# Modulation weights in quarters through two places of their own, a ring of five, a later turn of branch a

## The reference, cut to what matters

```
h = x @ w_in[i]                       # ua va za q k v zb ga gb, 18 column blocks of 512
ya = ua * sa * silu(za)               # branch a: a causal 128x128 mix over tokens
yb = rms(diff_attention(q, k, v)) * silu(zb)
merged = sigmoid(ga) * (ya @ w_branch_a) + sigmoid(gb) * (yb @ w_branch_b)
x = layer_norm(ALPHA * x + merged @ w_out + sigmoid(x @ w_ple_gate) * (p @ w_ple))
# second block: six modulation vectors of 1024 come from silu(c) @ w_mod + b_mod
# (1024 x 6144); attention with latents and with forget gates, then a mixture
# of 64 experts (6 a token) and a shared expert
```

## Time and profile before

| | us |
|---|---|
| median of 3 runs | 1123.41 (1122.72 to 1124.83) |
| the profiled execution, device time | 1123.09 |
| its span, first to last instruction | 1121.3 |
| TensorE busy, mean granted clock | 1059.9, 0.976 |
| VectorE, ScalarE, GpSimd busy | 546.5, 390.3, 338.4 |

### The profile page before, as it was taken

One profiled execution on the slowest core, in us unless ns is written; L12 is line 12 of the kernel. 1 busy time (PEld: TensorE's weight loads), 2 busy tenths in 40 slices (PEclk: granted clock), 3 DMA queues, 4 the chain that ended last, 5 costly groups with the idle time before them and its releaser, 6 DMA issues. The chain is left out here.

```text
span 1121.3 us, 12888 instructions
## 1 busy us (share of the span) xinstructions
PE 1059.9 (95%) x5022; PEld 705.2 (63%) x5022; DVE 546.5 (49%) x986; ACT 390.3 (35%) x677; POOL 338.4 (30%) x261
## 2 busy tenths in 40 slices
PE   6999999979999899799899999999999999999993
PEld 4888888868887787687678545444535354444442
DVE  5969676758757775855555222222222222212214
ACT  4645575446433654465233111111111111111112
POOL 1058965596486005918900000000000000000000
PEclk9999999989999899899999999999999999999997
DMA  9656654856766464454359499999999999999981
GB/s 328 209 175 243 215 188 147 315 174 224 247 216 210 153 195 155 166 171 148 113 216 414 192 392 412 420 416 417 416 416 418 417 418 416 416 417 417 417 362 39
DMA packets 93933, 320.65 MB, mean 286 GB/s; under 512 B 6288, under 2 KB 7328, under 8 KB 76976
## 3 DMA queue, kind: packets, MB, share of 16 engines
q1 hardware_dynamic: 92832, 316.07, 73.8%
q0 software_dynamic: 752, 3.22, 0.8%
q10 hardware_dynamic: 288, 0.52, 0.1%
HBM read 318.74 MB, written 1.05 MB: 285 GB/s over the span
## 5 line engine op out<-in xcount | busy, mean ns | idle before, releaser
L803 PE MATMUL ps<-hl,L 128*128 128x512 f32 (+1 forms) x1216 | 388.3, 401 | 14.4 <-DVE rlo L1615 8.5
L803 PEld LDWEIGHTS ps<-hl,L 128*128 128x128 f32 x1216 | 231.5, 193 | 63.7 <-issue 15.7
L1615 DVE TENSOR_TENSOR rlo<-ring,hl 128x1024 fp32r<-128x1024 f32 (+1 forms) x154 | 206.2, 1359 | 113.7 <-ACT hl L1241 113.3
L803 PE MATMUL ps<-rlo,L 128*128 128x512 f32 (+1 forms) x608 | 241.1, 396 | 0.0
L803 PE MATMUL ps<-slots_all,xe 128*64 128x512 f32 (+1 forms) x1056 | 226.9, 582 | 0.8 <-DVE rt L2406 0.8
L1241 ACT ACTIVATE hl<-ring 128x1024 fp32r<-128x1024 f32 (+1 forms) x154 | 158.8, 1055 | 182.5 <-PE ps L803 73.3
L764 POOL TENSOR_SCALAR ring<-ring,st 128x512 f32<-128x512 f32 x84 | 171.0, 2036 | 0.0
L792 POOL CAST two<-ident 64x128 fp32r<-64x128 f32 x64 | 18.7, 292 | 476.4 <-PE ps L803 440.7
L803 PEld LDWEIGHTS ps<-slots_all,xe 128*64 128x64 f32 x1056 | 73.9, 137 | 131.7 <-issue 128.5
L803 PEld LDWEIGHTS ps<-rlo,L 128*128 128x128 f32 x608 | 117.1, 193 | 24.9
L766 POOL TENSOR_TENSOR macc<-macc,ring 128x512 f32<-128x512 f32 x84 | 120.1, 1430 | 7.0
(11 more groups left out here) (210 smaller groups left out, 905.0 us busy)
## 6 DMA issues: line engine op xcount, KB each, us to landing
slots_all<-in_w_exp_gate SPq DMA_DIRECT2D x64, 1024.0 KB, 19.8
slots_all<-in_w_exp_up SPq DMA_DIRECT2D x64, 1024.0 KB, 15.8
slots_all<-in_w_exp_down SPq DMA_DIRECT2D x64, 1024.0 KB, 16.6
ring<-in_w_in SPq DMA_DIRECT2D x49, 1024.0 KB, 5.5
ring<-in_w_mod SPq DMA_DIRECT2D x24, 1024.0 KB, 5.2
ring<-in_w_out SPq DMA_DIRECT2D x8, 1024.0 KB, 5.1
ring<-in_w_ple_gate SPq DMA_DIRECT2D x4, 1024.0 KB, 5.1
ring<-in_w_branch_a SPq DMA_DIRECT2D x4, 1024.0 KB, 6.6
```

Source lines behind the costliest of these rows:

```text
L803: return e.matmul(o, l, r, start=start, stop=stop)
L1615: return e.tensor_tensor(o, a, b, op)
```

## The change

It takes the 24 modulation loads out of the ring's list. The ring has five places; the sixth becomes `mring`, two places of 512 KB. GpSimd queues the modulation weights itself, in 48 quarters of 512 KB (two rows of K), the next one into a place once its sums have left it. `MOD_SUM` is written out: most sums come one or two blocks earlier, part 11's from the end of the dense part to `om0`. The list of waits of GpSimd (the mask of `ws`, the second load of x into `rbuf`, the gates' bias) is hung on the parts 6, 8 and 5. Branch a is turned after `ga0` on all engines. The second load of `q0` comes in halves too, with a quarter of x ahead of each half, and the side job of the set-up starts after piece 4 and not piece 2. Five of the nine loads of constants wait for x's second quarter. TensorE starts with 12 matmuls of ones by ones into a bank that nobody reads. The expert loads start with the place of `mring`.

```diff
-NS = 6
+NS = 5
+WARM = 12
+        mring = place("mring", [128, 2, 1024])
-        for name in ("q0 q1 k0 k1 v0 v1 za0 m0 za1 ua0 m1 ua1 va0 m2 va1 aln zb0 ws zb1 m3 gb0 gb1 m6 ga0 ga1 m7 "
-                     "pg0 pg1 ple ba0 ba1 m8 bb0 bb1 m9 wo0 wo1 ln c0 fq fk up fv g0 m4 g1 m5 g2 g3 m10 of0 of1 "
-                     "om0 m11 om1 wp0 wp1").split():
+        for name in ("q0 q1 k0 k1 v0 v1 za0 za1 ua0 ua1 va0 va1 aln zb0 ws zb1 gb0 gb1 ga0 ga1 "
+                     "pg0 pg1 ple ba0 ba1 bb0 bb1 wo0 wo1 ln c0 fq fk up fv g0 g1 g2 g3 of0 of1 "
+                     "om0 om1 wp0 wp1").split():
-        place2 = [(len(loads) + q) % NS for q in range(NS)] + [11, 12, 6, 7, 8, 9, *range(13, NE), 10]
+        place2 = [5] + [(len(loads) + q) % NS for q in range(NS)] + [11, 12, 6, 7, 8, 9, *range(13, NE), 10]
+        MOD_SUM = {"ua0": [0], "va0": [1], "zb0": [2], "gb1": [3], "ga1": [6], "pg1": [7], "c0": [8], "fq": [9], "g1": [4],
+                   "g2": [5], "of0": [10], "om0": [11], "end": []}
+        in_turn = [c for v in MOD_SUM.values() for c in v]
+        def quarter_done(n):
+            return 15 * (n // 4) + 4 * (n % 4) + 3
-        AFTER = {"v0": "qT", "za0": "kT", "gb1": "yaT", "ba0": "ybT"}
+        AFTER = {"v0": "qT", "za0": "kT", "ga0": "yaT", "ba0": "ybT"}
-                if i == 0:
+                if i < 2:
+                    for q, s in enumerate((halves_in[i], slot_sem[i])):
+                        k = 2 * i + q
+                        e.dma_start(XTF[:, 2 * k:2 * k + 2, :], D["xT"][:, 2 * k:2 * k + 2]).then_inc(xt_in[k], 16)
+                        e.dma_start(slot(i)[:, 1024 * q:1024 * q + 1024].rearrange("p (a b) -> p a b", a=2),
+                                    src[:, 2 * q:2 * q + 2]).then_inc(s, 16)
+                elif j == 5:
+                    w.wait_ge(mac, quarter_done(nq - 1))
-            for dst, src in consts:
+            for n, (dst, src) in enumerate(consts):
+                if n == 4:
+                    w.wait_ge(xt_in[1], 16)
+            def quarter(n):
+                c, q = in_turn[n // 4], n % 4
+                e.dma_start(mring[:, n % 2, :].rearrange("p (a b) -> p a b", a=2),
+                            kn(D["w_mod"], 512 * c, 512 * c + 512)[:, 2 * q:2 * q + 2]).then_inc(mod_in[n % 2], 16)
+            w.wait_ge(pe_w, both(blocks["k0"][1]))
+            quarter(0)
+            quarter(1)
+            for n in range(nq):
+                if n % 4 == 0 and in_turn[n // 4] == 6:
+                    wsT_below()
+                if n % 4 == 0 and in_turn[n // 4] == 8:
+                    x_again()
+                if n % 4 == 0 and in_turn[n // 4] == 5:
+                    gate_bias()
+                for k in (0, 1):
+                    mod_part(n, 2 * (n % 4) + k)
+                if n + 2 < nq:
+                    w.wait_ge(mac, quarter_done(n))
+                    quarter(n + 2)
+            w.wait_ge(ones_set, 1)
+            for n in range(WARM):
+                mm(PS[7][:, 0:128], ones[:, :], ones[:, :], True, True)
-            for name in ("gb0", "gb1"):
+            for name in ("gb0", "gb1", "ga0"):
                 project(name, L0, x_ready)
             turn("yaT", lambda m, j: UA[:, m, 128 * j:128 * j + 128], lambda m, j0: w.wait_ge(ya_set, 2))
-            for name in ("ga0", "ga1", "pg0", "pg1"):
+            for name in ("ga1", "pg0", "pg1"):
                 project(name, L0, x_ready)
-                        if g > 1:
+                        if g > 3:
                             side.step(STEPS)
```

More of the change, by code:

```diff
@@ L212, in two_blocks @@
         GTV = st[:, 112:240].rearrange("p (m e) -> p m e", m=2)
-        loads, pieces, blocks, mods, once = [], [], {}, {}, {}
+        loads, pieces, blocks, once = [], [], {}, {}
         WI, W2 = D["w_in"], D["w_in_2"]
@@ L413, in read @@
             return ev.sem, ev.at[name]
[L417 to L425, removed]
+        MOD_SUM = {"ua0": [0], "va0": [1], "zb0": [2], "gb1": [3], "ga1": [6], "pg1": [7], "c0": [8], "fq": [9], "g1": [4],
+                   "g2": [5], "of0": [10], "om0": [11], "end": []}
+        in_turn = [c for v in MOD_SUM.values() for c in v]
+        nq = 4 * len(in_turn)
         before_mod = {c: q for q, c in zip(in_turn, in_turn[2:])}
-        assert all(q % 2 == c % 2 for c, q in before_mod.items())
+        def quarter_done(n):
+            return 15 * (n // 4) + 4 * (n % 4) + 3
         def aux_head(s):
@@ L575, in freed_by @@
                 return used[last_piece[i]] + 1
[L576 to L580, removed]
             after = {"aln": "zb0", "wsT": "zb1", "pT": "pg0", "ln": "wo1", "qup": "fv", "kvup": "fv"}[kind]
@@ L766, in mod_part, with wsT_below @@
                     e.tensor_tensor(acc, acc, v, ALU.add).then_inc(mac, 1)
[L768 to L784, removed]
+            def wsT_below():
+                i = once["wsT"]
+                w.wait_ge(slot_sem[i % NS], slot_at[i])
+                v = slot(i)[:, 0:1024].rearrange("p (g t) -> p g t", g=8)
+                e.affine_select(out=v, in_=v, compare_op=ALU.is_ge, fill=0.0, base=0, pattern=[[0, 8], [1, 128]],
+                                channel_multiplier=-1).then_inc(ws_set, 1)
@@ L1402, in _ @@
                 project(f"gb{c}", into(GB, c), ACT.Sigmoid, ("sa", 1, 1))
+            project("ga0", into(GA, 0), ACT.Sigmoid, ("s", 7, 1))
             rounded("yaT")
-            for c in range(2):
-                project(f"ga{c}", into(GA, c), ACT.Sigmoid, ("s", 7, 1))
+            project("ga1", into(GA, 1), ACT.Sigmoid)
             job = side.add(head_norm())
@@ L1977, in _ @@
                 project(name)
+            project("ga0")
             completed("yaT")
-            for name in ("ga0", "ga1"):
-                project(name)
+            project("ga1")
             job = side.add(head_norm())
```

40 lines of the change are left out of this document (17 added, 23 removed).

## The result

The changed kernel took 1111.68 us (median of 4 executions, 1111.39 to 1116.18), the kernel before 1123.54 beside it: ratio 0.9903, 95% interval 0.9888 to 0.9918, that is 11.9 us less. Run again with six executions (`e1_again`) it took 1113.66 against 1123.74, ratio 0.9919 [0.9898, 0.9940]. All ten have a median of 1113.4 and reach from 1111.4 to 1116.7. (The expectations of the later experiments put that median at 1112.5, which is 0.9 too low.) The forecast was 1109. Direction and range held; the way there did not, as the rest shows.

What follows compares the result with a forecast made beforehand. TensorE, busy 1059.9 of 1121.3 us, bounds the kernel, so only its losses in the first 600 us can pay; terms -3.7, 0, -9.0, -1, -2, +1.8, +0.5, -0.5, +1.0, -1.0 sum to -13.9: 1109 us, range 1099 to 1117.

Steps and rivals of the forecast that it cites:

- Start, -3.7: Before piece 2: halved loads with x in order remove a 2.0 us wait and 1.7 us of low clock.
- the warm-up: Twelve matmuls from 1.1 us on, ahead of the first piece: taken as 0, at best -1.5 us.
- Ring and branch a, -9.0: Stretch 226 to 241: with `ga0`'s load in time and the turn later, 9.0 us go; bounds -9.3 and -3.3.
- Rival (a): Branch a: the turn stays bound, `mod_sum(6)` waiting behind it; -9.0 becomes -3.3, 1115 us; chance 0.13.
- Rival (e): At `ga0`: `ws` and not the modulation delays the load, only the start pays; 1118 us; chance 0.05.
- Less contention, -1 and -2: At 338 to 350 and 500 to 560, GpSimd no longer disturbs VectorE: -1 (0 to -3.6) and -2 (0 to -5).
- GpSimd hidden: All GpSimd parts, at 7.2 us a quarter, end earlier than their sums, the closest by 24 us; new waits cost nothing.
- rival (d): At `om0`: TensorE waits for GpSimd's chain; at 14 us a quarter part 11 ends 30 us late, 1139 us; chance 0.04.
- Five places: +1.8, +0.5 and -0.5: Ring of five: `c0`'s first load later, +1.8; work ahead of `g0`'s exponentials, +0.5; one `wp1` load no longer late, -0.5.
- Rival (b): Ring of five: `c0` and `g0` cost their upper ends, +3 and +6; sum -7.2, 1116 us; chance 0.08.
- Sums moved: A small sum now uncovered at `fq` costs +1.0; the last part's sum leaving the chain to the router gives -1.0.

Runs made afterwards that it cites:

- thin sums: GpSimd works only the first row of K in full width, the other seven on 16 of 512 columns: kernel before 1103.22 us, changed kernel 1102.96 us.
- the old turn on the changed kernel: Changed kernel with the turn of branch a back between `gb1` and `ga0` on all engines: 1112.61 us, ratio 0.9909.
- the pause: Changed kernel, but GpSimd begins part 6 only when TensorE has done branch a's token mix: 1109.18 us, ratio 0.9882.
- thin sums on the old ring: Kernel before, GpSimd working only the first row of K in full width and the other seven on 16 of 512 columns: 1103.22 us, ratio 0.9825.

## Why the prediction was right, and where it was not

**The sum came out for reasons that cancel.** Forecast -13.9, measured -11.9 in the first comparison and some -10 over all executions. Eight microseconds at 180 to 203 were lost that no term of mine names, and about as many were won at `wo0` and `om0` above my terms.

**Start, -3.7: right.** -4.1 in two traces, 4.5 us by itself. The wait and the fall went as worked out: from the second piece to `q0` done after gains 3.9 (from -0.1 to -4.1) and so does the kernel without the warm-up (from +0.9 to -3.0). The 1 us between the two lies ahead of that, in when the clock rises. I took 0 for the warm-up and had bounded it by 1.5; its own share is not shown. What I missed is 1.2 to 1.5 us given back by `v0`. I had written that GpSimd "enters 42 to 68 ... where VectorE has room". The thin sums refute that: VectorE was the next bound there, and 2.6 to 2.9 us of the gain are left.

**Ring and branch a, -9.0: size right, cause in part.** -8.5 and -10.1 from `gb0` to `pg0`, with 70 matmuls in 226 to 241 as foreseen and 0.16 us of waiting ahead of `mod_sum(6)`. Rival (a), that the turn's chain stays bound, fell. The step that failed is that ring and turn act together: the old turn on the changed kernel costs nothing. Rival (e) fell as well. That part 3's sum left the place behind the turn, where it waited 3.01 us, I had as no term of its own, and it is not parted from the loads.

**Less contention, -1 and -2: mis-sized, since half the mechanism was missing.** The two stretches gained 5.1 and 6.4 us. In the first, contention is worth 1.8 by the thin sums, about my term; the other 3.4 I did not have, a load late by its place and a sum that left. In the second the load of `w_o_mla` stood behind modulation loads whose places GpSimd gave back late. I had read the ring at one place (`ga0`) and not looked for the same pattern, a weight load issued behind two modulation loads, at the two other stalls of the earlier trace rows.

**GpSimd hidden: right for TensorE, wrong for VectorE.** No wait of TensorE names a GpSimd operation, parts 3 to 9 ended 11 to 15 us after my times (3 by 176 where I had 165, 6 by 211 and not 196), a quarter taking mostly 7 to 9 us and at most 11 where I had 7.2, and rival (d) fell. But the loss to VectorE did not shrink by 3, it grew: the low parts' mean rose from 1359 to 1434 ns, as GpSimd now works without a gap through branch a's layer norm and on through the token mix. The price was +8; the pause takes 5.9 of it away. GpSimd is not the whole cause. In before it was as busy from 180 to 207 (24.09 us of 27) and TensorE waited 0.56 us in all, as VectorE had done the norm by 176. On the changed kernel VectorE waits 5.96 us for the late load of `zb1` and does the norm until 180, and then each slowed operation is paid. Up to the end of `zb1` a load in time and a silent GpSimd each remove the whole loss; behind it only GpSimd was tested cleanly. The same holds on a small scale ahead of `ba0`, +1.1 to +2.3 where I had 0: with thin sums it is 0. The rule of the Trainium skill that the prediction weighed (SBUF — State Buffer, "SBUF: two separate sides") is that one of the two engines holds a shared pair of ports for a whole instruction while the other waits; from it I had drawn that more even work moves the loss and does not remove it. The slower rows, 3.71 against 2.48 us, agree with it that the engines hinder each other; no run here shows the lock itself. Where the loss reaches TensorE only the timeline says. The prediction listed where GpSimd leaves and where it enters, and for 156 to 181 it said again that VectorE has room, from a mean over the stretch: it did not look at what waits for VectorE there.

**Five places: +1.8, +0.5 and -0.5: mis-sized, and two places missed.** `c0` +2.7 to +3.0, `g2` first +0.8 to +1.3, `wp1` -1.3. Missed were `fv`, +1.5 to +2.0, with ScalarE waiting 5.00 us for the load ahead of it in `e1_again`, and the load of `zb1`, which is issued at 162.56 and not at 157.52, while `aln` and `ws` hold two of the five places (with `ws` behind it ScalarE has its first piece 9 us sooner). At `g0` thin sums on the old ring win 5.4, and the changed kernel, with GpSimd gone from there, loses 0.4 to 0.9. By difference the ring's share is about 6, as I had it. But no run changes the number of places alone, so what I put down to the ring here is argued and not shown. Rival (b) came true at `c0`, at its upper end, and not at `g0`.

**Sums moved.** At `fq` +2.2, not +1.0: I took the 2.08 us of sixteen products for two sums, and it is one. At the end +1.1 to +1.4, not -1.0: I had counted an instruction as on the path because it stood in front of one, without asking whether that one waited for it.

## What to carry to other kernels

Before an engine is given more even work, list for each stretch what waits for the engine that it disturbs; a stretch with idle time in the mean can hold a chain in which every slowed operation is paid in full. A pause there pays if the sums have slack: here it gave 5.9 us and cost 1.6 later. Look also at why the disturbed engine is late, as a load in time can make the same disturbance harmless. A short instruction inside a wait is free, and taking it out can cost the clock: in the seven traces with 6.8 us of low clock at the router the sum was gone. When one stall is explained by a queue, look for the same order of issues at every other stall before giving those another cause.

## What the runs showed of the hardware

GpSimd's elementwise work on 128 x 512 beside VectorE's cost the kernel before 20.8 us of 1124, more than all that the change brought: 226 us less of GpSimd's time gave that much of the program's, 5.3 of it where GpSimd held places of the ring. The same wait of 1.94 us ahead of the last pair's second products was followed by the low clock in before's trace and not in `e1_again` (0.62 and 1.00 over 4.5 us). At `ba0` an idle stretch of 1.99 us was followed by it in after (0.54 over 3.7 us), and one of 2.28 us in the pause was not (1.00 over 10.4 us). One kernel's executions spread over 5 us. Twelve small products from 1.1 us on, ended by 5.7, still left the first real ones at the low clock at 8.6 (1.19 us for two), and the clock rose for good at 11.4; in other traces with them it was up from 7 us on, or only from 14.2, and in the four traces without them it rose between 11.2 and 14.6.
